# Hybrid encoder, one core: the D skip product moves from ScalarE to GpSimd, and two VectorE steps change places

## The reference

```python
xbc = jax.nn.silu(depthwise_conv_centred(xbc, conv_w, conv_b))
xs, Bm, Cm = jnp.split(xbc, [D_INNER, D_INNER + N_GROUPS * D_STATE], axis=-1)
...
y_f = ssd_chunked(xs, dt_f, A[0], Bm, Cm)
y_b = flip(ssd_chunked(flip(xs), flip(dt_b), A[1], flip(Bm), flip(Cm)))
y = y_f + y_b + xs.astype(jnp.float32) * d_skip[:, None]
y = y.reshape(b, s, D_INNER) * jax.nn.silu(z.astype(jnp.float32))
yg = y.reshape(b, s, N_GROUPS, D_INNER // N_GROUPS)
yg = yg * lax.rsqrt(jnp.mean(jnp.square(yg), axis=-1, keepdims=True) + RMS_EPS)
```

## Time and profile before

| | before |
|---|---|
| median of 3 runs | 2511.32 us (2508.12 to 2515.46) |
| the profiled execution | 2515.46 us, span of its instructions 2513.5 us |
| granted TensorE clock, mean | 0.993 |
| PE, PEld, DVE, ACT, POOL busy | 2433.3, 1961.4, 1482.1, 1340.9, 601.0 us |
| memory traffic | 405.69 MB, 161 GB/s over the span |

### The profile page before, as it was taken

The page is one execution under the profiler, slowest core; times in us unless marked ns, Lnnn a source line. Parts: engine busy times, 40 slices in busy tenths (PEclk is TensorE's granted clock), DMA queues, the critical chain, the costliest instruction groups (busy, mean ns, idle before and its releaser), DMA issues.

```text
span 2513.5 us, 34992 instructions
## 1 busy us (share of the span) xinstructions
PE 2433.3 (97%) x11436; PEld 1961.4 (78%) x11436; DVE 1482.1 (59%) x2563; ACT 1340.9 (53%) x1802; POOL 601.0 (24%) x717
## 2 busy tenths in 40 slices
PE   7999999999999999999999999999999999999997
PEld 6878788887777788887678787878877868888865
DVE  5799898999643311012658989989895351111126
ACT  5655656365564644344556456654646555444454
POOL 2424333142111111111124143432421101111110
PEclk9999999999999999999999999999999999999999
DMA  7567484747788589889564756757577867888883
GB/s 194 129 152 155 109 184 105 173 118 150 169 183 209 126 193 195 187 197 208 129 158 101 175 115 154 171 111 160 117 167 162 207 151 174 191 197 187 194 198 100
DMA packets 110700, 405.69 MB, mean 161 GB/s; under 512 B 12288, under 2 KB 12288, under 8 KB 110208
## 3 DMA queue, kind: packets, MB, share of 16 engines
q0 software_dynamic: 54144, 197.16, 46.7%
q1 hardware_dynamic: 55296, 202.66, 24.2%
q10 hardware_dynamic: 1152, 4.37, 0.5%
HBM read 402.04 MB, written 2.10 MB: 161 GB/s over the span
## 4 chain that ended last, share of the span: by engine, by line
PE 68%; DVE 14%; ACT 9%; issue 6%; DMA 3%; POOL 1%; ACTq 0%; DVEq 0%; SPq 0%; POOLq 0%
PE bank L750 20%; PE bank L752 20%; PE bank L751 20%; DVE tmp_m L1196 3%; DMA w_raw<-w_stream 2%; ACT w_lo L425 2%; ACT w_hi L424 2%; DVE tmp_m L1192 1%; PE bank L889 1%; PE bank L792 1%; PE bank L793 1%; DVE tmp_y L1164 1%; PE bank L795 1%; DVE y_tok L1223 1%; DVE tmp_y L1221 1%
## 5 line engine op out<-in xcount | busy, mean ns | idle before, releaser
L328 POOL DMA_DIRECT2D w_lo<-w_stream x376 | 327.9, 878 | 1588.6 <-ACT w_lo L425 1532.3
L750 PE MATMUL bank<-x_hi,w_hi 128*128 128x512 f32 x1728 | 686.0, 397 | 7.9 <-DMA w_lo<-w_stream 7.9
L752 PE MATMUL bank<-x_hi,w_lo 128*128 128x512 f32 x1728 | 675.9, 391 | 0.0
L751 PE MATMUL bank<-x_lo,w_hi 128*128 128x512 f32 x1728 | 675.2, 391 | 0.0
L424 ACT ACTIVATE w_hi<-w_raw 128x1024 fp32r<-128x1024 f32 x378 | 398.1, 1053 | 304.7 <-PE bank L752 241.6
L425 ACT ACTIVATE w_lo<-w_raw 128x1024 fp32r<-128x1024 f32 x378 | 395.8, 1047 | 0.0
L750 PEld LDWEIGHTS bank<-x_hi,w_hi 128*128 128x128 f32 x1728 | 325.6, 188 | 80.0 <-issue 12.3
L751 PEld LDWEIGHTS bank<-x_lo,w_hi 128*128 128x128 f32 x1728 | 325.5, 188 | 71.0 <-issue 3.3
L752 PEld LDWEIGHTS bank<-x_hi,w_lo 128*128 128x128 f32 x1728 | 325.4, 188 | 68.9
L1114 DVE SCALAR_TENSOR_TENSOR z_a<-glu_out,conv_a_params,z_a 128x497 f32 (+14 forms) x480 | 320.7, 756 | 0.0
L1480 DVE TENSOR_TENSOR glu_out<-bank,sigmoids 128x512 f32<-128x512 f32 x44 | 30.5, 692 | 414.1 <-PE bank L752 414.1
(11 more groups left out here) (213 smaller groups left out, 3669.5 us busy)
## 6 DMA issues: line engine op xcount, KB each, us to landing
w_raw<-w_stream SPq DMA_DIRECT2D x378, 512.0 KB, 5.0
w_lo<-w_stream POOLq DMA_DIRECT2D x376, 512.0 KB, 7.4
z_b<-x_in SPq DMA_DIRECT2D x4, 512.0 KB, 5.7
w_ple_in<-w_ple ACTq DMA_DIRECT2D x2, 1024.0 KB, 10.4
out<-z_b SPq DMA_DIRECT2D x1, 2048.0 KB, 6.3
ple_p<-p_in ACTq DMA_DIRECT2D x2, 512.0 KB, 5.8
params<-par_in ACTq DMA_DIRECT2D x2, 340.0 KB, 3.0
tmp_m<-w_dt ACTq DMA_DIRECT2D x2, 256.0 KB, 5.2
```

The source lines that it names most:

```text
L328: gp.dma_start(wlo[:, s, :], w_stream[cyc, s].bitcast(F32R), accum_op=ALU.add).then_inc(lo_done[s], 16)
L750: pe.matmul(dst, wh, mh, start=first, stop=False)
L751: pe.matmul(dst, wh, ml, start=False, stop=False)
L752: return pe.matmul(dst, wl, mh, start=False, stop=last)
```

## The change

GpSimd gets a `skip` of its own: one `tensor_tensor` multiply over 128x1024 elements, `x_tok` by the four factors of `group_skip` broadcast over chunks and over the 64 values of a head. ScalarE's `skip`, four instructions a group, goes away. GpSimd runs it for G0 behind `masked_steps(0, G0, 3)`, for G1 behind `masked_steps(1, G0 + 1, 3)`, each time ahead of a `lo`. The wait for `grp_ready` is not repeated, since GpSimd has waited for it already. On VectorE, G1's `mix` of chunk 1 now stands ahead of `weighted_xs` for the last state product.

```diff
         @block.gpsimd
         def _(gp):
-            open_(gp, rhs_ready, rms_done, zb_zero)
+            open_(gp, rhs_ready, xd_ready, rms_done, zb_zero)
...
+            def skip(q, G):
+
+                gp.wait_ge(tok_evac, seen(3 * G + 2))
+                gp.wait_ge(yt_done, seen(2 * G))
+                d = gdsk[:, q, :].unsqueeze(1).unsqueeze(3).broadcast_to([P, CH, HG, HEAD])
+                v = "p c (h e) -> p c h e"
+                gp.tensor_tensor(y[:, :, :].rearrange(v, h=HG), xtok[:, :, :].rearrange(v, h=HG), d,
+                                 ALU.mult).then_inc(xd_ready, 1)
...
                     masked_steps(0, G0, 3)
+                    skip(0, G0)
                     lo(c0 + 3, 0, 1)
...
                     masked_steps(1, G0 + 1, 3)
+                    skip(1, G0 + 1)
                     lo(c0 + 4, 0, 1, 2, 3)
...
         @block.scalar
...
-            def skip(q, G):
-
-                act.wait_ge(tok_evac, seen(3 * G + 2))
-                act.wait_ge(grp_ready, seen(G + 1))
-                act.wait_ge(yt_done, seen(2 * G))
-                for h in range(HG):
-                    e = slice(h * HEAD, (h + 1) * HEAD)
-                    i = act.activation(y[:, :, e], xtok[:, :, e], ACT.Copy, scale=gdsk[:, q, h:h + 1])
-                i.then_inc(xd_ready, 1)
...
                 b_tokens(G0)
-                skip(0, G0)
...
                 decay(G1, 2)
-                skip(1, G1)
                 state(G1, 2)
...
                     glu(c0 + 3, 0, 0)
+                    mix(1, G1, 1)
                     weighted_xs(1, G1, 2)
-                    mix(1, G1, 1)
                     entering(1, G1)
```

More of the change, by code:

```diff
@@ L413, in _ @@
         def _(act):
-            open_(act, xh_done, silu_done, tok_evac, xd_ready, exp_done, st_evac, ss_done, yh_done,
+            open_(act, xh_done, silu_done, tok_evac, exp_done, st_evac, ss_done, yh_done,
                   sq_ready, std_ready, zf_ready, zh_ready, bh_done, fh_done,
```

## The result

The changed kernel took 2547.43 us, the median of four runs (2543.57 to 2549.84), beside 2510.08 us for the kernel before on the same chip (2508.12 to 2515.46). The ratio is 1.0144, with a 95% interval from 1.0129 to 1.016: 1.4% slower, 36 us by the ratio (37 between the two medians). The forecast was 2534 us with a range to 2548, so the sign is right, and the size lies 0.6 us inside the upper end of the range. The changed kernel's profiled execution took 2544.5 us with a span of 2541.8.

What follows compares the result with a forecast made beforehand. Mostly TensorE-bound, but VectorE's lateness at G1 delays TensorE equally. ScalarE 0, G0 0, G1 2.0 plus 0.8 make 2.8 us a pair, 22 us for eight; from the 2511.3 median, 2534 us, range 2516 to 2548.

Steps and rivals of the forecast that it cites:

- The chain: Second pair's waits: from TensorE at G0's state products over ScalarE and VectorE, back to TensorE only at G1's transposes, 303.30.
- ScalarE's relief: Removing ScalarE's four activations a group gains 0; as a rival, it saves 13 us, giving 2498, chance 0.04.
- The multiply's length: One GpSimd multiply per group takes 2.2 us, between 1.1 and 3.3.
- G1's hold: At G1 the multiply holds VectorE for 92% of 2.2 us, 2.0 us a pair, between 0.5 and 3.3.
- The partial hold: Rival: at G1 VectorE loses only 45% of 2.2 us, 1.0, plus 0.8: 14 us, 2526, chance 0.22.
- GpSimd giving way: Rival: the multiply is stretched, VectorE isn't held, 0 to 0.8 us a pair remain: 2511 to 2518, chance 0.14.
- G0, predicted 0 and at most 0.7: The multiply behind G0's chunk 3 selections costs nothing, at most 0.7 us if a 3.3 us multiply delays G1's selections.
- The slack of 3.5 us: At G0, VectorE's 2.08 us wait for ScalarE's states copy and the selections' hold until 243.79, beside one product.
- is held until 243.79 by the next selections in any case: At G0, after waiting for ScalarE's states copy, VectorE is held by GpSimd's next selections regardless of the multiply.
- The exchange: G1's mix of chunk 1 ahead of weighted_xs: TensorE waits 1.6 us, VectorE loses 0.8 us a pair.
- fits in what it waits anyway: At G1, TensorE's lateness of 1.6 or 3.6 us is absorbed by waits of 0.41 and 1.7, plus 2.8.
- The wait before G1's transposes: TensorE's wait for VectorE's normalised y_tok, 1.7 us a pair, 13.5 in eight; expected grown or moved.

Runs made afterwards that it cites:

- The doubling experiment: Kernel before plus the GpSimd multiply in both groups, VectorE's order unchanged, with G1's multiply done twice, first into an idle tensor: 2542.48 us, ratio 1.0128.
- The fills: Kernel before without ScalarE's skip product; at the multiply's places GpSimd does two memsets that write as many elements and read nothing: 2511.48 us, ratio 1.0001.
- The multiply alone: Changed kernel with weighted_xs back in its old place ahead of G1's mix of chunk 1, multiply on GpSimd in both groups: 2525.94 us, ratio 1.0055.
- the exchange alone: Kernel before with only G1's mix of chunk 1 moved ahead of weighted_xs, ScalarE keeping the skip product: 2520.23 us, ratio 1.0034.
- the multiply too early: Kernel before plus the GpSimd multiply in both groups, VectorE's order unchanged, G1's multiply ahead of chunk 1's selections: 2594.83 us, ratio 1.0327.

## Why the prediction was right, and where it was not

*What bounds a pair.* The chain was misread in one point: it doesn't come back to TensorE only at the transposes. Between ScalarE at 271.86 us and VectorE at 274.82 it goes over two pieces of TensorE (272.51, 0.65 us, and 273.16, 1.03 us). For the stretch of G1's half, from 274.82 on, the reading holds, and the forecast didn't use the other part.

*ScalarE's relief, predicted 0: right.* With all 64 activations gone and nothing that reads in their place, the ratio is 1.0001. TensorE's banks still set when ScalarE starts. Its row behind the place of G0's activations, and the one behind G1's, answer to the earlier trace rows:

```profile
236.24 0.60 ACT L441 ACTIVATE conv_in<-bank 128x512 f32<-128x512 f32 x1 [4.28 <-PE bank L751]
...
294.68 0.60 ACT L477 ACTIVATE states<-bank 128x512 f32<-128x512 f32 x1 [6.42 <-PE bank L851]
```

The idle time grew from 2.70 to 4.28 us and from 1.43 to 6.42.

*The multiply's length, predicted 2.2 us: right at G0, 0.3 us too long at G1.* It measured 2.23 us at G0 and 1.92 at G1. The Trainium skill (GPSIMD Engine Reference, section "3.1 Elementwise — side-by-side cycle accounting") gave 2.25 as an estimate, half of its figure for 2048 elements; the trace agrees at G0 and is 0.3 below it at G1.

*G1's hold, predicted 2.0 us: right in kind, 1.55 measured.* It falls on the step of 284.01 that was named, which took 2.18 us, 1.49 more. The working took 92% of the multiply. But the product began 0.3 us behind the multiply, a shorter one than assumed, and what it lost is the rest of it: 1.92-0.29 = 1.63 was left, and it lost 1.49, again about 92%. The doubling experiment shows that a second multiply costs as much again. The partial hold, 1.0 us by 45%, is ruled out at this step. Its 45% was also reckoned on another base than the 92%: of what the selections had left when the small steps began at 281.37, 2.37 us, the loss of 1.38 is 58%. At G0 the small steps lose 1.5 us of the 1.71 that the multiply had left, 88%. So in these rows the multiply held VectorE nearly whole, and it was the selections, four instructions in a row, that held the small steps in part. GpSimd giving way is ruled out by the length, 1.92 us at that very place.
The Trainium skill (SBUF — State Buffer, section "Who interferes with whom") says that a VectorE instruction with two SBUF inputs contends with a GpSimd instruction that reads SBUF, and not with one that only writes. The fills against the multiply agree: 0.69 us beside the one, 2.18 beside the other. The order that the prediction took from that section, that the one that starts second is blocked, doesn't agree everywhere: the product of 239.16 us in the version with G0's multiply alone and the convolution's step of 227.59 started 0.10 and 0.16 us ahead of GpSimd's instruction, and they were held.

*G0, predicted 0 and at most 0.7: 0.6 measured.* The slack of 3.5 us was set against one product's hold. The multiply lengthened the small steps by 1.5 us, and that moved a step into reach of the next selections, whose hold of 2.7 us then also counted. The step that failed is "is held until 243.79 by the next selections in any case": they hold whichever step VectorE is in, and now it was an earlier one.

*The exchange, predicted 0.8: 1.25 measured*, alone and inside the sum. The two waits were worked out exactly, 1.64 and 0.84 us. Of the other 0.4, the rows show 0.09 in the overlap that the wait breaks and 0.17 in the small steps of `mix`, which the exchange moves fully beside the selections. The prediction had "the same work in the same time" there. The last 0.15 stays open.

*The step that failed for the size* is the sentence that TensorE's own lateness "fits in what it waits anyway". Two things were wrong in it. It counted the wait and not what follows: TensorE's wait ahead of the last state product came out at 3.13 us in every pair (3.6 was worked out, with a hold 0.5 longer than measured), and at it the granted clock fell in five of eight. And it set TensorE's lateness against waits that come after `y_chunk`. The multiply alone shows that this is sound for lateness that begins at `y_chunk`'s later chunks: the 1.7 us before the transposes took it in. But VectorE needs the last state product and the first products of `y_chunk` at once, so what TensorE loses there passes through VectorE to the end and never meets that slack. The pairs with a fall behind the state product are 1.5 us longer than the others.

The terms by what the runs showed: G0 0.6, G1's hold 1.55, the exchange 1.25, together 3.4 us a pair; in five of eight pairs 1.5 more. That is 8x3.4+5x1.5 = 35 us, beside 36 measured; the prediction had 8x2.8 = 22. Of the 12 us between the two sums, 7.5 are the clock, 4.8 are G0's, and G1's hold and the exchange, off by 0.45 us in opposite directions, cancel by luck. It is luck as well that the range held the time, by 0.6 us: the upper bounds of the terms reached far enough, and nothing in it allowed for the clock.

The wait before G1's transposes, which I had as a possible place for the loss, kept its size in the changed kernel, 13.1 us in eight against 13.5: VectorE sets the end there before and after.

## What to carry to other kernels

Work that moved to GpSimd and reads SBUF was paid for here by VectorE, 1.5 us for a multiply of 1.92, where VectorE's steps beside it had both inputs in SBUF, and it cost nothing beside a step with an input from a bank. So look for such a place in GpSimd's order, and count every step that the multiply and the selections behind it may meet. When an edit makes TensorE wait for some microseconds, reckon with a fall of the granted clock in some of the repetitions (five pairs of eight at 3.13 us here), and price it by who waits for the matmuls right behind: nothing (the multiply alone) where a wait of TensorE's own, 1.7 us, took it in, and 1.5 us (the change) where VectorE, which sets the end, needed them at once. And read a new wait in an in-order queue by what stands behind it: the same multiply cost nothing at one place of GpSimd's list and over 3% two entries earlier.

## What the hardware showed that was not expected

- *TensorE's clock is lost to a few microseconds of waiting in the midst of full work, and the wait's length alone doesn't tell when.* In the kernel before it falls in no pair. At a wait of 4.42 us it fell in eight pairs of eight, at 3.13 us in five, at 1.94 us (the doubled multiply) in four, behind 1.44 us late in the pair in four of eight, behind two waits of 0.78 and 0.63 us (the version in which TensorE takes the state product later) in two, behind 1.64 us (the exchange alone) in none. Equal waits at equal places thus had different outcomes, and the second pair, in which the change was read, is one of the three that kept the clock: one pair can't tell this. The Trainium skill (TensorE: Matmul & The Clock Gate, section "HAM oscillation — how this bites in real kernels") describes the same loss for waits on DMA. The version with the multiply too early agrees, with the clock at 0.50 around waits of 5.59 to 7.2 us for weights in all eight pairs; in the others the waits were on VectorE or on ScalarE's copy.
- *The hold goes both ways, even between the same two kinds of instruction.* At 216.64 us the first of four selections was stretched to 3.96 us and left the convolution alone; ten microseconds later in the same kernel selections held the convolution's steps, 1.11 us instead of 0.74, and the multiply held one for its whole length, 2.94 us. What decides between the two was not tried.
- *GpSimd's fills*, 128x1024 elements in 0.95 us, left VectorE's product beside them at 0.69 us.
